# A pad of 128 bytes in on-chip memory between the weights' buffers and everything allocated behind them

## What is computed

```python
for i in range(DEPTH):                                   # DEPTH = 2
    h = rms_norm(x, attn_norm[i])
    proj = h @ w_in[i]                                   # 1024 x 3072
    y = concat(stick_breaking(...), differential(...))
    x = x + y @ w_out[i]                                 # 1024 x 1024
    h2 = rms_norm(x, ffn_norm[i])
    x = x + (swiglu(h2, gate, up, down)                  # 2816 wide
             if i == 0 else moe_swiglu(h2, ...))         # 8 experts, 3584 wide
return rms_norm(x, final_norm)
```

## Time and profile before

| | |
|---|---|
| median of 3 runs | 1421.14 us (1420.51 to 1421.22) |
| the profiled execution, its own time | 1421.18 us |
| its span, first to last instruction | 1418.1 us |
| PE busy | 1401.5 us (99%) |
| DVE busy | 1125.9 us (79%) |
| ACT busy | 935.7 us (66%) |
| granted TensorE clock, mean | 0.997 |
| memory traffic | 316 GB/s over the span |

### The profile page before, as it was taken

The page is one execution under the profiler, slowest core; times in us unless marked ns, Lnnn a source line. Parts: engine busy times, 40 slices in busy tenths (PEclk is TensorE's granted clock), DMA queues, the critical chain, the costliest instruction groups (busy, mean ns, idle before and its releaser), DMA issues.

```text
span 1418.1 us, 18353 instructions
## 1 busy us (share of the span) xinstructions
PE 1401.5 (99%) x6935; PEld 1169.0 (82%) x6935; DVE 1125.9 (79%) x852; ACT 935.7 (66%) x758; POOL 36.9 (3%) x52
## 2 busy tenths in 40 slices
PE   8999999999999999999999999999999999999997
PEld 8878888889888888888888888888888888888885
DVE  5865544546856999988888888898888888889897
ACT  5555444435555777777777777777777777777775
POOL 0010000000010020000000000000000000001200
PEclk9999999999999999999999999999999999999999
DMA  9734985555424999999999999999999999999992
GB/s 333 258 117 135 395 307 184 184 190 179 149 90 143 353 390 396 396 393 391 355 395 394 352 386 379 379 368 376 395 346 397 392 353 389 388 373 356 396 396 111
DMA packets 190908, 448.80 MB, mean 316 GB/s; under 512 B 8516, under 2 KB 11403, under 8 KB 190859
## 3 DMA queue, kind: packets, MB, share of 16 engines
q1 hardware_dynamic: 188890, 441.74, 85.1%
q0 software_dynamic: 1648, 5.78, 1.1%
q10 hardware_dynamic: 320, 0.60, 0.1%
HBM read 429.74 MB, written 18.36 MB: 316 GB/s over the span
## 4 chain that ended last, share of the span: by engine, by line
PE 98%; DVE 1%; ACT 1%; DMA 0%; issue 0%; DVEq 0%; ACTq 0%
PE ps L515 90%; PE ps L956 2%; PE ps L638 1%; PE ps L596 1%; PE ps L662 0%; PE ps L915 0%; PE ps L685 0%; PE ps L791 0%; PE ps L520 0%; DMA cst<-in_consts 0%; PE ps L627 0%; PE ps L649 0%; PE ps L651 0%; PE ps L926 0%; PE ps L650 0%; PE ps L639 0%
## 5 line engine op out<-in xcount | busy, mean ns | idle before, releaser
L365 DVE TENSOR_TENSOR w_lo<-raw,w_hi 128x2048 fp32r<-128x2048 f32 x401 | 914.9, 2290 | 211.2 <-ACT w_hi L360 210.0
L360 ACT ACTIVATE w_hi<-raw 128x2048 fp32r<-128x2048 f32 (+1 forms) x401 | 766.9, 1914 | 306.0 <-PE ps L515 302.6
L515 PE MATMUL ps<-w_hi,xe_hi 128*128 128x512 f32 x896 | 247.0, 397 | 0.0
L515 PE MATMUL ps<-w_lo,xe_hi 128*128 128x512 f32 x896 | 241.8, 392 | 0.0
L515 PE MATMUL ps<-w_hi,xe_lo 128*128 128x512 f32 x896 | 240.7, 391 | 0.0
L515 PEld LDWEIGHTS ps<-w_lo,xe_hi 128*128 128x128 f32 x896 | 168.3, 188 | 37.4
L515 PEld LDWEIGHTS ps<-w_hi,xe_lo 128*128 128x128 f32 x896 | 168.3, 188 | 37.1
L515 PEld LDWEIGHTS ps<-w_hi,xe_hi 128*128 128x128 f32 x896 | 164.7, 188 | 32.8
L515 PE MATMUL ps<-w_hi,he_hi 128*128 128x512 f32 x448 | 122.2, 394 | 0.0
L515 PE MATMUL ps<-w_lo,he_hi 128*128 128x512 f32 x448 | 121.2, 392 | 0.0
L515 PE MATMUL ps<-w_hi,he_lo 128*128 128x512 f32 x448 | 120.7, 391 | 0.0
(11 more groups left out here) (244 smaller groups left out, 977.8 us busy)
## 6 DMA issues: line engine op xcount, KB each, us to landing
raw<-in_expert_w_gate SPq DMA_DIRECT2D x112, 1024.0 KB, 7.3
raw<-in_expert_w_up SPq DMA_DIRECT2D x112, 1024.0 KB, 7.6
raw<-in_expert_w_down SPq DMA_DIRECT2D x112, 1024.0 KB, 7.3
raw<-in_w_in SPq DMA_DIRECT2D x24, 1024.0 KB, 6.0
raw<-in_dense_w_gate SPq DMA_DIRECT2D x11, 1024.0 KB, 7.1
raw<-in_dense_w_up SPq DMA_DIRECT2D x11, 1024.0 KB, 8.2
raw<-in_dense_w_down SPq DMA_DIRECT2D x11, 1024.0 KB, 4.9
raw<-in_w_out SPq DMA_DIRECT2D x8, 1024.0 KB, 5.3
```

The source lines that it names most:

```text
L360: nc.scalar.activation(w_hi[:, n % SPL, 0:width], raw[:, n % RAW, 0:width], ACT.Copy).then_inc(hi_ready, 1)
L365: nc.vector.tensor_tensor(w_lo[:, n % SPL, :], raw[:, n % RAW, :], w_hi[:, n % SPL, :].bitcast(F32), ALU.subtract).then_inc(lo_ready, 1)
L515: return pe.matmul(o, stationary, moving, start=start, stop=stop, skip_group_check=True)
```

## The change

One tile is allocated behind `w_lo` and used by nobody: 32 float32 numbers, 128 bytes of each partition. No instruction is added, removed or moved on any engine; only the start addresses of the tiles behind it grow by 128, and with them the address fields of the instructions that use them.

```diff
         raw = sb("raw", [P, RAW, PIECE])
         w_hi = sb("w_hi", [P, SPL, PIECE], F32R)
         w_lo = sb("w_lo", [P, SPL, PIECE], F32R)
+        shift_rows = sb("shift_rows", [P, 32])
         xs = sb("xs", [P, TT, D])
         hn = sb("hn", [P, TT, D])
```

## The result

The changed kernel takes 1444.39 us (median of 4 runs, 1443.26 to 1444.64) against 1421.07 us (4 runs, 1420.51 to 1421.22): a ratio of 1.0162, 95% interval 1.015 to 1.0174. The forecast of no difference was wrong. The time lies inside the range, at the price of the slower rival.

A forecast was written before the change was run, and what follows sets the result against it. The prediction took PE's matmul count times pace as the bound, 5160 x 228.9 ns = 1181 us being touchable. Its likeliest case added 0 to the profiled time, giving 1421.1 us, with a range of 1390 to 1446 us.

The forecast's parts named there:

- The forecast of no difference: Whole kernel: pace of the large matmuls unchanged at 228.9 ns, time 1421.1 us; given 38%.
- the slower rival: 512-column matmuls: each gets the step scatter shows, +4.4 ns, 22.7 us in all, 1444 us; chance 26%.
- What bounds the kernel: PE: number of matmuls times start-to-start pace sets the end; one nanosecond of pace is worth 5.2 us.
- DVE, ACT, DMA at nothing: Other engines and transfers: their large work's tiles stay put, slower small operations would be hidden; cost nothing.
- The value that I take is ... zero change, by the row that is nearest: 512-column matmuls: pace always 228.9 ns after every kind of entry, so zero change was taken.
- two bounds: New 512-column pace: upward +4.4 ns from scatter; downward -4.4 ns, or -8.7 ns by ratio, from the 256-column paces.
- The rival faster by one step: 512-column matmuls: -4.4 ns each, as the 256-column places suggest, together -20.8 us, 1400 us; chance 28%.
- Its count of fast matmuls: columns_out: 528 of 768 matmuls taken as fast, losing 4.4 ns each, +2.3 us at most.
- "Modulo 512": Operand addresses taken modulo 512 bytes: moving against stationary 128 against 64 before, 128 against 192 after.
- The rule of separate ports: PE: loading the next weights takes no bandwidth from the running matmul, hence no change, 38%.

The follow-up runs named there:

- the second sweep: Matmul stretches alone, without the computation, varying widths, d (stationary less moving operand's address), held moving operand and stepped addresses; 256 columns held at +64 gave 113.3 ns.
- the sweep: Matmul stretches alone, without the computation, varying d (stationary less moving operand's address): 512 columns took 226.8 to 234.3 ns, 256 columns 117.3 to 120.1 ns.

## Why the prediction was wrong, point by point

- **What bounds the kernel: right.** The end is the count of matmuls times their pace; 4.4 ns on 5160 of them moved the time by 23 us, and one nanosecond of pace is worth what was said, 5.2 us, to within a tenth.
- **DVE, ACT, DMA at nothing: right.** Their durations are unchanged, and with all tiles moved together the time is that of before.
- **"The value that I take is ... zero change, by the row that is nearest": this step failed.** Its reason was that the pace is 228.9 ns after every kind of entry. But all those entries have one value of d, so they say that the pace is stable at d = -64, and nothing of another d. The comparison that varied d, `rest_out` behind transposes against `columns_out` behind transposes, did show an effect. It was set aside for the reason that operands alternate in different orders there; the second sweep shows that holding the operand doesn't matter and d does. Within the kernel, too, both places changed their pace with d and not with their order: `rest_out` went to 113.3 to 113.6 ns and `columns_out` to 117.7. In place of zero the runs showed +4.4 ns on each of the 5160 matmuls. Zero was not the nearest row; it was a retreat to the middle of two bounds that both were off zero.
- **The rival faster by one step: its mechanism is real, its sign for 512 columns was not.** It carried the order of two differences from 256 columns to 512, and the sweeps show that the order is another there. Where it spoke of 256 columns it was right, as the same two places show. (Its count of fast matmuls was too high by 16, which ran at 117.8 ns before as well; that is 0.1 us.)
- **The rival slower: its price was right, to 1 us, by luck.** Its row was misread: `scatter` ran at 233 ns at d = 0, and d = 0 in a long run is one of the two best differences, 226.8 ns. A stretch at d = 0 in the sweep begins, behind its first step, with 231, 235, 229, 232 and 231 ns and then falls to 227; `scatter` has runs of four matmuls and never gets there. At d = -64 in the kernel before, the second to fourth steps of the 89 runs also take 231 to 234 ns. So the +4.4 ns agree with what d = +64 costs, but nothing in that row could have told it, and that the time lies inside the stated range rests on this rival alone. Of its mechanism the condition came true, the stationary operand above the moving one is bad for 512 columns, but so is d = 224, which is -32 with the stationary operand below: it is one of many bad differences, and that the two reads "meet most" there is shown by no run.
- **"Modulo 512" was the wrong period:** 256 bytes do, for every difference tried in steps of 32 bytes.
- **The rule of separate ports** was named in the prediction as the source of the no-change case, from the Trainium skill's page "TensorE: Matmul & The Clock Gate", section "Step-by-step: what each phase is for". What the prediction took from it, that the addresses of the two reads can't matter to each other, doesn't hold for float32r here: moving only the address difference changes the pace of a stream with nothing else running, 226.8 to 234.3 ns. Whether the weight load takes bandwidth from the stream, which is what the page denies, no run shows. The prediction's one sign of agreement, that DVE's and ACT's work leaves the pace alone, says nothing of PE's own two reads.

## What to carry to other kernels

Where PE is busy all the time and streams float32r, read its pace from the starts of long runs and compare it with the columns at the granted clock; if it is some per cent above, the difference of the two operands' addresses modulo 256 bytes is worth a sweep, and two pads of 64 bytes at the right tiles gave 0.6% here. The best difference found still stands 6% above the columns at the clock, so not all of the distance can be won this way. An allocation in front of such tiles (a new small buffer, a changed size) cost 1.6% here without any instruction being different, so a change that also moves addresses has to be compared at equal differences. Evidence for "this knob does nothing" needs rows in which the knob has different values; many rows at one value are none.

## What the runs showed of the hardware that was not expected

- float32r, 128 stationary and 512 moving columns, back to back: 226.7 to 234.3 ns by the address difference modulo 256 bytes, against 215.8 ns for bfloat16 and 213.3 for one column a cycle at the 2.4 GHz level. The good differences found are 0 and -16 (226.7 to 226.8) and -64 (228.9); all others tried in steps of 16 bytes lie between 229.8 and 234.3.
- The best difference depends on the width: for 256 columns it is +64, 113.3 ns, with 117.8 as a second stable pace at the same addresses (`columns_out` in the kernel before), and 0 is among the worst, 120.0.
- For 512 columns the differences -64 and +64 keep their pace at four places 128 bytes apart, and with or without the other engines' work and traffic.
- What in PE's reads makes this was not found: the loss doesn't follow the number of stationary columns, stays near 13.3 ns between 256 and 384 moving columns at d = 0, and stepped addresses don't mix the paces of fixed ones.
